# A two-block transformer kernel on one core: token quarters by way of DRAM, sums formed in place, the last gate group as quarter products, a root and the index rounding moved

## The reference, cut to what matters

```python
h = rmsnorm(x, norm_g[l])
(a_q, a_ckv, i_q, i_k, i_w, a_gate, b_q, b_k, b_v, b_gate,
 c_q, c_gate, mix_gate) = split_cols(h @ w_in[l], IN_SIZES)
...
qa = rmsnorm(a_q.reshape(bsz, seq, A_HEADS, A_HEAD_DIM), q_norm_a[l])
oa = dsa_attention(qa, ka, va, iq, ik, iw, bias_a, topk) * jax.nn.silu(a_gate)
# inside dsa_attention, the indexer:
rel = jax.nn.relu(jnp.einsum('bthd,bsd->bths', iqb, ik))
score = jnp.einsum('bths,bth->bts', rel, iwb)
```

## Time and profile before

| what | value |
|---|---|
| median of three runs | 2502.67 us (2500.90 to 2502.89) |
| the profiled execution's own time | 2501.32 us |
| its span, first to last instruction | 2499.6 us |
| mean granted clock of TensorE | 0.998 |
| PE busy | 2481.5 us, 99% |
| VectorE, ScalarE, GpSimd busy | 57%, 32%, 25% |
| DMA | 443.95 MB, mean 178 GB/s |

### The profile page before, as it was taken

How to read it: one execution, slowest core, us unless ns; L and a number is a source line. 1 busy time by engine, 2 the same in 40 slices (tenths; PEclk the granted TensorE clock), 3 DMA queues, 4 the chain that set the end, 5 groups by cost and what they waited for, 6 DMA issues and landing times.

```text
span 2499.6 us, 35254 instructions
## 1 busy us (share of the span) xinstructions
PE 2481.5 (99%) x13180; PEld 2078.5 (83%) x13180; DVE 1423.2 (57%) x2381; ACT 798.6 (32%) x1177; POOL 624.0 (25%) x795
## 2 busy tenths in 40 slices
PE   9999999999999999999999999999999999999998
PEld 7788799998888888888888888888888888888886
DVE  5673977973337985545554333555555455455525
ACT  7422444443333432233222122323232222233221
POOL 0213655640011232322000220221222333343100
PEclk9999999999999999999999999999999999999999
DMA  7547233443345676778444453666656545546622
GB/s 276 173 154 198 101 129 125 135 152 118 123 165 187 237 249 221 246 245 288 168 167 151 143 159 121 181 213 195 204 188 202 185 157 165 182 153 205 242 99 101
DMA packets 99959, 443.95 MB, mean 178 GB/s; under 512 B 17622, under 2 KB 17622, under 8 KB 71750
## 3 DMA queue, kind: packets, MB, share of 16 engines
q1 hardware_dynamic: 38712, 241.58, 27.6%
q0 software_dynamic: 61136, 200.86, 25.7%
HBM read 347.27 MB, written 96.59 MB: 178 GB/s over the span
## 4 chain that ended last, share of the span: by engine, by line
PE 96%; DVE 2%; DMA 1%; issue 1%; SPq 0%; POOL 0%; ACT 0%; DVEq 0%; ACTq 0%; POOLq 0%
PE bank L446 24%; PE bank L447 24%; PE bank L448 24%; PE bank L863 10%; PE bank L1214 5%; PE bank L1137 2%; PE bank L1275 2%; PE bank L1116 2%; PE bank L1006 1%; PE bank L982 1%; DMA w_raw<-wst 1%; PE bank L945 1%; DVE t_x L2034 0%; PE bank L1001 0%; PE bank L977 0%
## 5 line engine op out<-in xcount | busy, mean ns | idle before, releaser
L435 DVE TENSOR_TENSOR w_lo<-w_raw,w_hi 128x2048 fp32r<-128x2048 f32 x178 | 409.4, 2300 | 411.5 <-ACT w_hi L430 407.0
L430 ACT ACTIVATE w_hi<-w_raw 128x2048 fp32r<-128x2048 f32 x177 | 338.8, 1914 | 550.2 <-PE bank L448 475.3
L446 PE MATMUL bank<-act_b,w_hi 128*128 128x512 f32 x1280 | 502.2, 392 | 0.0
L447 PE MATMUL bank<-act_b,w_lo 128*128 128x512 f32 x1280 | 499.0, 390 | 0.0
L446 PE MATMUL bank<-act_a,w_hi 128*128 128x512 f32 (+1 forms) x1256 | 494.9, 394 | 4.0 <-DVE w_lo L435 4.0
L448 PE MATMUL bank<-act_b,w_hi 128*128 128x512 f32 x1280 | 498.7, 390 | 0.0
L448 PE MATMUL bank<-act_a,w_hi 128*128 128x512 f32 (+1 forms) x1256 | 490.3, 390 | 0.0
L447 PE MATMUL bank<-act_a,w_lo 128*128 128x512 f32 (+1 forms) x1256 | 490.2, 390 | 0.0
L446 PEld LDWEIGHTS bank<-act_b,w_hi 128*128 128x128 f32 x1280 | 240.4, 188 | 54.4 <-issue 5.2
L446 PEld LDWEIGHTS bank<-act_a,w_hi 128*128 128x128 f32 (+1 forms) x1256 | 236.1, 188 | 55.5 <-issue 5.8
L448 PEld LDWEIGHTS bank<-act_b,w_hi 128*128 128x128 f32 x1280 | 240.4, 188 | 50.2
(11 more groups left out here) (364 smaller groups left out, 2994.8 us busy)
## 6 DMA issues: line engine op xcount, KB each, us to landing
w_raw<-wst SPq DMA_DIRECT2D x210, 1024.0 KB, 5.0
prob_t<-flip_d POOLq DMA_DIRECT2D x64, 512.0 KB, 4.8
flip_d<-flip POOLq DMA_DIRECT2D x56, 512.0 KB, 4.7
mix_d<-stage POOLq DMA_DIRECT2D x24, 512.0 KB, 2.9
mixg<-mix_d POOLq DMA_DIRECT2D x8, 1536.0 KB, 6.8
prob_tk<-flip_d POOLq DMA_DIRECT2D x32, 256.0 KB, 5.7
flip_d<-flip_a POOLq DMA_DIRECT2D x16, 512.0 KB, 2.9
b<-rows_2d POOLq DMA_DIRECT2D x16, 448.0 KB, 10.3
```

What stands on the lines that cost most here:

```text
L430: act.activation(w_hi[s][:], w_raw[s][:], ACT.Copy).then_inc(hi_ready, 1)
L435: dve.tensor_tensor(w_lo[s][:], w_raw[s][:], w_hi[s][:].bitcast(F32), ALU.subtract).then_inc(lo_ready, 1)
L446: pe.matmul(out_ap, l_hi, r_hi, start=start, stop=False)
L447: pe.matmul(out_ap, l_lo, r_hi, start=False, stop=False)
```

## The change

The scaled tokens are stored in DRAM while they are made (`x_d`, four buffers `tr_h` in place of two, in the first 8 KB of the staging area), and GpSimd's eight additions are replaced by eight loads of quarters from there. The loads go to the places where the hi parts will be (`x_raw_q`), the sums to the places of the lo parts (`x_raw_t`), and the rounding and the subtraction work in place. On VectorE all four sums of a half come together, then `mem_keys_out`, then the four lo parts, then the lo parts of chunks 26 and 27. Group 13 uses banks 3 and 5. Group 27 becomes a group of quarter products, with its loop ends. The root moves to group 21, the rounding of the index keys and queries and the zeroing of `score` into group 27, and the index products wait for group 27's results to be read.

```diff
-G_S0, G_S1 = G_Q + 2, G_GATE + 7
+G_S0, G_S1 = G_Q + 2, G_MIX
+    x_d = nc.dram_tensor("x_d", [KT, P, T], F32).ap()
-        tr_h = [sb_at(f"tr_h{i}", [P, T], Y + 20 * KB + 2 * KB * i) for i in range(2)]
+        tr_h = [sb_at(f"tr_h{i}", [P, T], Y + 2 * KB * i) for i in range(4)]
-        x_sum = [sb_at(f"x_sum{i}", [P, 4, 256], Y + 12 * KB + 4 * KB * i) for i in range(3)]
+        x_raw_q, x_raw_t = [[[sb_at(f"{name}{i}{n}", [P, 4, 256], RB + 32 * KB * i + 8 * KB * n + 4 * KB * h) for n in range(4)]
+                             for i in range(2)] for h, name in enumerate(("x_raw_q", "x_raw_t"))]
...
@@ TensorE
-            b0 = 0 if g % 2 else 5
+            b0 = 5 if g % 2 else 0
-            proj(G_Q + 1, (2, 3), lambda: ssq(0, 0))
+            proj(G_Q + 1, (3, 5), lambda: ssq(0, 0))
-            proj(G_S1, (2, 4))
-                    pe.wait_ge(ev_dve, G_MIX - 1)
+                    pe.wait_ge(gc_s, RD0 + 8)
...
@@ ScalarE
-            act.wait_ge(kst_v, 256)
-            act.wait_ge(brow_out, 48)
             split_hi(act, 2 * G_Q + 1, 1)
-            for n in range(3):
+            for n in range(4):
                 x_sum_hi(0, n)
             split_hi(act, 2 * G_Q + 2, 0)
-            x_sum_hi(0, 3)
+            split_hi(act, 2 * G_Q + 3, 1)
             q_out(0)
-            split_hi(act, 2 * G_Q + 3, 1)
-            act.wait_ge(kst_k, 256)
             for n in range(4):
                 x_sum_hi(1, n)
...
                     split_hi(act, 2 * G_S1, 0)
+                    act.wait_ge(pt_used, PB0 + 6 * (2 * G_S1 - 1 - C_S0) + 5)
+                    copy(ik_parts[0][:], ik_t[:]).then_inc(tt_s, 1)
+                    idx_query_hi(0, 0)
...
+                if g == G_GATE + 1:
+                    act.wait_ge(rq_s, 1)
+                    act.activation(ssq_q[:], rq[:], ACT.Sqrt).then_inc(rt_s, 1)
-            hi2(G_S1)
-            summed(G_S1)
             act.wait_ge(ev_dve, G_S1 - 1)
-            act.activation(th_g[:, 0, :], bank[2][:], ACT.Tanh, scale=0.5).then_inc(gth, 1)
-            act.activation(th_g[:, 1, :], bank[4][:], ACT.Tanh, scale=0.5).then_inc(ev_act, 1)
-            act.wait_ge(rq_s, 1)
-            act.activation(ssq_q[:], rq[:], ACT.Sqrt).then_inc(rt_s, 1)
...
@@ VectorE
-                if i >= 2:
-                    dve.wait_ge(tt_s, i - 1)
-                    dve.wait_ge(tl_s, i - 1)
+                if i >= 4:
+                    dve.wait_ge(tt_s, i - 3)
+                    dve.wait_ge(tl_s, i - 3)
+                    dve.wait_ge(x_stored[i % 4], 16 * (i // 4))
...
             def x_sums(c):
-                b11, b12, b22 = x_sum
-                dve.wait_ge(xs_b, X0 + 4 * c + 3)
-                dve.tensor_tensor(b11[:], b12[:], b11[:], ALU.subtract).then_inc(xs_t, 1)
-                ...
+                (b11, b12, b22, b21), (t1, t3, t2, t4) = x_raw_q[c], x_raw_t[c]
+                dve.wait_ge(xq_loaded[c], 64)
+                dve.tensor_tensor(t1[:], b12[:], b11[:], ALU.subtract).then_inc(xs_t, 1)
+                dve.tensor_tensor(t3[:], b22[:], b12[:], ALU.subtract).then_inc(xs_t, 1)
+                dve.wait_ge(xs_t, X0 + 4 * c + 1)
+                if c:
+                    dve.wait_ge(kst_k, 256)
+                dve.tensor_tensor(t2[:], b22[:], t1[:], ALU.subtract).then_inc(xs_t, 1)
+                dve.wait_ge(xs_t, X0 + 4 * c + 3)
+                dve.tensor_tensor(t4[:], t2[:], b21[:], ALU.subtract).then_inc(xs_t, 1)
...
             split_lo(dve, 2 * G_Q + 1, 1)
-            dve.wait_ge(kst_v, 256)
-            dve.wait_ge(brow_out, 48)
             x_sums(0)
             mem_keys_out()
+            for n in range(4):
+                x_sum_lo(0, n)
             split_lo(dve, 2 * G_Q + 2, 0)
-            for n in range(3):
-                x_sum_lo(0, n)
-            x_last_sum(0)
-            x_sum_lo(0, 3)
+            split_lo(dve, 2 * G_Q + 3, 1)
             q_out(0)
-            split_lo(dve, 2 * G_Q + 3, 1)
-            dve.wait_ge(kst_k, 256)
             x_sums(1)
-            for n in range(3):
+            for n in range(4):
                 x_sum_lo(1, n)
-            x_last_sum(1)
-            x_sum_lo(1, 3)
             part_w_lo(C_S0, range(7))
             q_out(1)
...
+                    dve.wait_ge(chunk_used, 2 * G_S1 - 1)
+                    dve.memset(score[:], 0.0).then_inc(zero_s, 1)
                     dve.wait_ge(pt_used, PB0 + 6 * (2 * G_S1 - 1 - C_S0) + 4)
                     split_lo(dve, 2 * G_S1, 0)
+                    dve.wait_ge(tt_s, IQ0)
+                    dve.tensor_tensor(ik_parts[1][:], ik_t[:], ik_parts[0][:].bitcast(F32), ALU.subtract).then_inc(tl_s, 1)
+                    idx_query_lo(0, 0)
...
@@ GpSimd
             pool.memset(warm[:], 0.0).then_inc(warm_s, 1)
+            for i in range(KT):
+                pool.wait_ge(th_s, i + 1)
+                pool.dma_start(x_d[i], tr_h[i % 4][:]).then_inc(x_stored[i % 4], 16)
...
             def x_quarters(c):
-                (three x_quarter additions with waits)
+                for n, k, half in ((1, 0, 1), (0, 0, 0), (2, 1, 1), (3, 1, 0)):
+                    a = CK * c + 4 * k
+                    pool.dma_start(x_raw_q[c][n][:], x_d[a:a + 4, :, 256 * half:256 * half + 256].rearrange("n p t -> p n t"))\
+                        .then_inc(xq_loaded[c], 16)
...
             pool.wait_ge(kst_v, 256)
             pool.wait_ge(brow_out, 48)
+            for b in range(4):
+                pool.wait_ge(x_stored[b], 64)
             x_quarters(0)
+            pool.wait_ge(kst_k, 192)
+            x_quarters(1)
             bias_rows(rows_n, rpb_in.rearrange("h r c -> h (r c)"))
             pool.wait_ge(sp_o, 8)
             for h in range(HEADS_C):
                 pool.dma_start(k_d[6 + h, :, 0:256], kt_c[:, h, :]).then_inc(kst_k, 16)
-            x_last_quarter(0)
-            x_quarters(1)
             proj_store(G_Q)
-            x_last_quarter(1)
-            pool.wait_ge(kst_k, 256)
-            pool.wait_ge(xs_lo, SQ0 + 8)
             w_sums(C_S0)
```

More of the change, by code:

```diff
@@ L394, in build_kernel @@
         PROB2_T0 = 64
-        ol_s = [sem(f"o_loaded{i}") for i in range(6)]
+        ol_s = [sem(f"x_moved_and_o_loaded{i}") for i in range(6)]
+        x_stored, xq_loaded = ol_s[0:4], ol_s[4:6]
         oh_s, olo_s = sem("o_hi"), sem("o_lo")
@@ L1432, in _ @@
             split_hi(act, 2 * G_IQ + 3, 1)
+            for b in range(4):
+                act.wait_ge(x_stored[b], 64)
             iq_out(G_IQ, 0)
@@ L1586, in part_hi @@
                 k0, k1 = parts[p]
-                act.wait_ge(ol_s[p], 16 * loads)
+                act.wait_ge(ol_s[p], 16 * loads + 64)
                 copy(act_b[0][:, k0:k1, :], o_raw[:, k0:k1, :]).then_inc(oh_s, 1)
@@ L1966, in _ @@
             split_lo(dve, 2 * G_IQ + 3, 1)
+            for b in range(4):
+                dve.wait_ge(x_stored[b], 64)
             iq_out(G_IQ, 0)
@@ L2119, in _ @@
                     gate_out(g)
-            split_lo(dve, 2 * G_S1 + 1, 1)
-            dve.memset(score[:], 0.0).then_inc(zero_s, 1)
-            split_lo(dve, 2 * G_S1 + 2, 0)
-            summed(G_S1)
-            dve.wait_ge(staged_out[1], 160)
-            for n_, (sm, v) in enumerate(((gth, 1), (ev_act, G_S1))):
-                dve.wait_ge(sm, v)
-                last = dve.scalar_tensor_tensor(out=stage[1][:, n_, :], in0=th_g[:, n_, :], scalar=1.0,
-                                                in1=bank[2 + 2 * n_][:], op0=ALU.add, op1=ALU.mult)
-            last.then_inc(ev_dve, 1)
-            def idx_query_lo(t, par):
-                dve.wait_ge(tt_s, IQ0 + t + 1)
-                dve.tensor_tensor(iq_lo[par][:], qb1[par][:], iq_hi[par][:].bitcast(F32), ALU.subtract).then_inc(tl_s, 1)
             dve.wait_ge(zero_s, 1)
-            dve.wait_ge(tt_s, IQ0)
-            dve.tensor_tensor(ik_parts[1][:], ik_t[:], ik_parts[0][:].bitcast(F32), ALU.subtract).then_inc(tl_s, 1)
-            idx_query_lo(0, 0)
             def idx_dve(i, last=False):
```

77 lines of the change are left out of this document (26 added, 51 removed).

## The result

| | median us | runs | profiled execution | its span |
|---|---|---|---|---|
| before | 2502.78 (2500.9 to 2506.5) | 12 | 2501.32 | 2499.6 |
| after | 2509.07 (2506.14 to 2511.55) | 12 | 2508.83 | 2507.2 |

The ratio is 1.0027, 95% interval 1.0019 to 1.0034: slower, by 6.3 us, where no change (2501.0) was forecast. The time lies outside the forecast's range, which ended at 2507.

What follows compares the result with a forecast made beforehand. PE, busy for 99% of the span, was taken to bound the kernel. Token quarters +0.4, last gate group -1.7 and root and index rounding -0.4 sum to -1.7, taking 2502.67 to 2501.0 us; range 2492 to 2507.

Steps and rivals of the forecast that it cites:

- Stores of the 16 scaled tiles: GpSimd's x_d stores during scaling, with mem_vn's and twelve tiny stores moved behind them: 0 us, bounds 0 to 3.6.
- Loads of the token quarters: Around chunks 26 to group 14, loads replace GpSimd's sums: 7.8 wait plus 1.6 clock less 9.0, net +0.4 us.
- the low clock: PE running partly at 1.2 GHz instead of 2.4 after the new wait at chunk 26: 1.6 us lost.
- the old stalls: PE's excess time from 261.49 to 292.11 us, around chunk 27 and group 14: 9.0 us, expected to go.
- L: Time when the first four token quarters are there for VectorE: forecast 245 us, from bytes queued at 412 GB/s.
- change = L - 246.7: Whole change in us as a line in the quarters' landing time; breaks even at a landing of 246.7.
- The Trainium skill's rule: A GpSimd DMA takes 2.0 us plus bytes at 436 GB/s; would make the token-quarter part -9.0 us.
- Last gate group: Group 27 as quarter products takes 20.2 us instead of 21.9 on PE: -1.7 us.
- Root and index rounding: Start of index stage: no table load before ScalarE's first Relu, w_hi 1.3 us earlier: -0.4 us, bounds -0.6 to +1.
- Scaling held up by its stores: Rival: slow stores delay tile scaling and PE, +3.6 us, 2504.6 us; chance 0.06.
- Loads in time: Rival: token quarters land at 237 to 240, little or no PE wait, at best -11.1, 2491.6 us; chance 0.27.
- slow loads: Rival: 1 KB pieces slow the token quarters; at 104 GB/s they land at 257, 2513 us; chance 0.10.

Runs made afterwards that it cites:

- tiny_front: The kernel after with the twelve 64-byte stores issued ahead of the sixteen x_d stores instead of behind them: 2513.35 us, ratio 1.0048.
- tiny_later: The kernel after with the twelve 64-byte stores issued behind the stores of v_nat, from 142 to 148 us: 2502.41 us, ratio 1.0001.
- best2: The kernel after with twelve tiny stores behind v_nat's, first quarters loaded earlier, splits of chunks 26, 27 and part of 28 moved ahead: 2492.05 us, ratio 0.9960.

## Why the prediction was wrong

- *Stores of the 16 scaled tiles, taken at 0.* The step that failed. The stores themselves were 0, as said: no wait of VectorE on them, no wait of PE from 60 to 96 us, 13.94 us at 114 in tiny_front and tiny_later. But the step also moved mem_vn's and twelve tiny stores "back to after the last tile, and nothing before group G_IQ reads their semaphores", and priced them by who waits for *them*. Nobody does. What they cost is what they do to the loads beside them, 5.7 us in the profile, 6.0 to 6.7 in the medians (tiny_later against the kernel after). With them out of the way the kernel has 2502.4, 1.4 from the forecast. The row that could have told it was there: chunk 12's load, 8.5 us beside the same stores in the kernel before.
- *Loads of the token quarters, +0.4, bounds -9.0 and +12.5.* The mechanism held in each link (a new wait at chunk 26 on w_lo, the low clock behind it, the old stalls gone, 8.9 for 9.0). One size was off: L was 248.1, not 245. Its bytes were to be through at 244.3; a mean rate of 379 GB/s in place of 412 adds 1.2 us and the second four quarters, which the count of bytes left out although it had them issued at 237.5, 2.7. The wait was 10.4 for 7.8, the low clock 1.9 for 1.6, the part +3.5. The line "change = L - 246.7" with the measured L gives +1.4; the rest of the 7.6 is the tiny stores and the +0.8 of the first 60 us, within 0.3.
- The Trainium skill's rule (DMA: Bandwidth & Descriptors, "Anatomy of one DMA — SWDGE (gpsimd) path") by which, as an estimate, 2.10 MB issued from 230.1 would be in at 236.9, did not hold: the same four loads took 11.1 to 15.0 us each. Even with rows_2d out of the way the last took 10.4.
- *Last gate group, -1.7.* Measured -1.6: its 168 matmuls run at 120 ns, and PE waits for nothing behind them.
- *Root and index rounding, -0.4.* Measured -0.7: 18.31 us from the first index product to the second block (585.19 to 603.50), for 18.98 before (576.82 to 595.80); no table load before the first Relu, as assumed.
- *Scaling held up by its stores*: did not happen; the stores landed in 2.3 to 7.9 us, and VectorE waited for none.
- *Loads in time*, the rival with 0.27, did not happen. That its 2491.6 is near best2's 2492.05 is its price coming true without its condition: in best2 the last quarter landed at 242.3 on the clock of the kernel before, later than the rival's 240, and it is the order on VectorE that takes the wait away.
- The chances: I gave 0.14 to slower: about 0.05 by slow loads, which did not decide it, and the rest to what I had not seen in a reordered program, which is what came. The range ended 2 us short, since it held no term for a move of DMAs past others.

## What to carry over

When an edit moves a DMA, ask not only who waits for it but which transfers run beside it at the new place, however few bytes it has; here it was enough to make the dummy stores 512 bytes long or to put them where two chunks of weights were already in. When a new source is later than the old one, look at what stands behind it in each engine's list: moving two splits ahead of the sums gained 13.6 to 14.6 us here, while issuing the loads 8 us earlier, ahead of two other kinds of stores, gained 8.9 to 9.5, since a slow store filled the engines for most of that time. And when bytes are counted up to a landing, those issued before it belong in the count too.
